# Heads stage of a hybrid attention block: VectorE instead of ScalarE copies the turned probabilities

## Chip, cores and metric

One Trainium2 chip, one of its cores. The metric is the device time of one execution in microseconds (us). The kernel before takes 2724.59 us, the median of 3 runs (2723.51 to 2724.68). The engines are called PE (TensorE), DVE (VectorE), ACT (ScalarE), POOL (GpSimd) and SP (SyncE). PEld is PE's weight load, which overlaps its matmuls.

## The reference, cut to what matters

```python
for start in range(0, S, Q_BLOCK):          # S = 512, Q_BLOCK = 128: four query blocks, b = 0..3
    end = start + Q_BLOCK                   # block b sees 128 * (b + 1) keys
    ...
    # differential heads (8 of them, "kind 0"): two softmaxes and their difference
    p = probs(q1, k1) - lam * probs(q2, k2)
    outs.append(jnp.einsum('bhqk,bhkd->bhqd', p.astype(v.dtype), v[:, :, :end]))
    ...
    # forgetting heads (8 of them, "kind 1"): one softmax
    p = jax.nn.softmax(logits, axis=-1)
    outs.append(jnp.einsum('bhqk,bhkd->bhqd', p.astype(v.dtype), v[:, :, :end]))
```

Around this stand the input projection with RMS norms of queries and keys (`h @ w_in`, then `rms_norm` per head), the gates, the branch projections, the output projection and an MLP. All is float32, 512 tokens by 2048 features.

## The kernel before, in words

The kernel is a chain of stages. In each of them PE multiplies with float32 weights that were split into a rounded high part (by ACT) and a remainder (by DVE), as three products. This case is about the heads stage, from about 490 us to 1010 us of the span.

**Turns and units.** The stage has eight turns (`heads_turn`, a Python call for turn 0 and a hardware loop for turns 1 to 7) and a tail that has the same shape. A turn computes queries and keys of one differential and one forgetting head: 16 units (u = 0 to 15), each of 12 matmuls of 128x512 (L1678, L1680, L1681). The weights of a unit pass through one of four slots: `round_unit` on ACT (L671, once PE has used the slot four units before), `split_unit` on DVE (L1109), then the unit on PE. ACT and DVE prepare unit u+3 in step u.

**Steps of the heads, hung between the units.** `head_hooks` adds to each unit the steps of the heads that are under way. The differential head of turn i has its steps t = 0 to 31 in units 0 to 15 of turn i and 0 to 15 of turn i+1; the forgetting head of turn i has t = 0 to 7 in units 8 to 15 of turn i and t = 8 to 23 in turn i+1. So in unit u of a turn, the head before (differential) is at t = u+16, the head before (forgetting) at t = u+8, and the new differential head at t = u. On every engine the order is the one written out: there is no planner, and each engine takes its instructions strictly in that order.

For query block b of a head the steps are:
- PE `take_scores` (L1723; L1728 and L1730 for the differential head) at SOFTMAX_STEPS[b] = 14, 15, 17, 19, into the PSUM banks `scores`.
- DVE `take_logits` in the same step: adds the bias and takes the row minimum (L1185, after a small memset L1182).
- ACT exponential in the same step (L698).
- DVE `take_probs` one step later (reciprocal L1198; L1201 and L1204 for a differential head, L1207 for a forgetting head).
- PE `turn_probs` at TURN_STEPS (16, 17, 20, 22 for differential and 16, 17, 19, 21 for forgetting heads): b+1 transposes of 128x128 into the one PSUM bank `turned` (L1740). It waits for the probabilities, and for the copy of the block before, since there is one bank.
- `keep_turned` in that same step, on ACT (L717): copies 128 x 128(b+1) float32 from `turned` to SBUF, and raises `p_keys_ready`.
- PE multiplies with the values at PV_STEPS (23 and 22), after the copies of all four blocks (L1778: four matmuls of 512, 384, 256 and 128 columns, each of which the trace records as two).

**Norms.** The new head's queries and keys are normed in the same units: squares on ACT (L678), turned on PE (L1689), reduced on DVE (L1143), a chain of 12 small dependent instructions on DVE (`rsqrt`, L1126 to L1132), widened on PE (L1705), multiplied on DVE (L1167). For the differential head, ACT then rounds (L733) and DVE splits (`split_step`, L1248: two halves for queries, four for keys); PE's first scores of the head (t = 14) wait for that.

**Order within one step on DVE**: products with the widened norm (`scale_step`), then `head_step` of the three heads, then `split_step`, `split_unit`, and at last `norm_step` (reduction and chain). Inside `head_step`, all `take_probs` come first, then for b = 0 to 3 `take_logits(b)`.

**Order within one step on PE**: the heads' hooks come ahead of the unit: for one head, the norm's turns, then scores, then `turn_probs`, then the product with the values.

Of the kernel before, what the change touches and what calls it, by code (L numbers as in the profile page):

```python
# [22 lines left out]
ACT = mybir.ActivationFunctionType  # L23
ALU = mybir.AluOpType

P = 128
# [8 lines left out]
TURN_STEPS = ((16, 17, 20, 22), (16, 17, 19, 21))  # L35
# [14 lines left out]
def at_least(eng, sem, value):  # L50

    if not (isinstance(value, int) and value <= 0):
        eng.wait_ge(sem, value)
# [29 lines left out]
def tile(tensor, m):  # L83

    return tensor[:, m] if isinstance(m, int) else tensor[:, bass.ds(m, 1)].rearrange("p a s -> p (a s)")
# [12 lines left out]
def build(nc, x, w_in, b_forget, w_branch_diff, w_branch_fox, w_gate, w_out, w_mlp_up, w_mlp_down,  # L98
          x_tiles, columns, out):
    _, S, D = x.shape  # L100
    assert x.shape[0] == 1 and w_in.shape[0] == 1 and S == 512
    DT = D // P
    TB = S // P
# [38 lines left out]
    with ExitStack() as ctx:  # L142
# [84 lines left out]
        with ExitStack() as third:  # L227
# [31 lines left out]
        p_blocks = [main_flat[:, p_at + P * b:p_at + P * b + p_stride * (b + 1)].rearrange("p (j c) -> p j c", c=p_stride)  # L259
                    for b in range(TB)]  # L260
# [15 lines left out]
        turned = ctx.enter_context(nc.psum_tensor("turned", [P, S], F32))  # L276
# [384 lines left out]
        def _(act):  # L661
# [22 lines left out]
            def head_step(kind, i, t, work):  # L684

                if t == BIAS_STEP and kind == 1:

                    act.wait_ge(f_wide, i + 1)
                    for b in range(TB):
                        nc.scalar.activation(bias_fox[:, bias_at[b]:bias_at[b + 1]], scores[1][:, 0:P * (b + 1)],  # L690
                                             ACT.Identity, scale=-1.0,
                                             bias=neg_f[:, b, bass.ds(i, 1)]).then_inc(bias_open, 1)
                for b, when in enumerate(SOFTMAX_STEPS):
                    if t == when:
                        block_no = i * (2 * TB) + TB * kind + b
                        act.wait_ge(logits_ready, block_no + 1)
                        for m in range(2 - kind):
                            e = nc.scalar.activation(logits[m][:, 0:P * (b + 1)], logits[m][:, 0:P * (b + 1)],  # L698
                                                     ACT.Exp, scale=-1.0, bias=row_min[:, m:m + 1],
                                                     accum_out=row_sum[:, m:m + 1])  # L700
                        e.then_inc(exp_ready, 1)
                if kind == 1 and t == 22:

                    act.wait_ge(pv_ready, i * 2 + 2)
                    nc.scalar.activation(tile(b_hi, i + H), heads_out[:, :], ACT.Copy).then_inc(o_hi, 1)
                for b in range(TB):
                    if t == TURN_STEPS[kind][b]:
                        keep_turned(kind, i, b)

            def keep_turned(kind, i, b):  # L710


                block_no = i * (2 * TB) + TB * kind + b
                act.wait_ge(probs_turned, block_no + 1)

                at_least(act, pv_ready, i * 2 + kind)
                nc.scalar.activation(p_blocks[b][:, :, 0:P],  # L717
                                     turned[:, 0:P * (b + 1)].rearrange("p (j q) -> p j q", q=P),
                                     ACT.Copy).then_inc(p_keys_ready, 1)

            def norm_step(kind, i, t, work):

# [164 lines left out]
            def heads_turn(i, work):  # L887
                for u in range(HU):
                    round_unit(work, u + LEAD)
                    if isinstance(i, int) and i == 0 and u == 2:  # L890
                        act.wait_ge(lam_sums, 1)
                        nc.scalar.activation(lam[:, 2:4], stats[:, 0:2], ACT.Exp).then_inc(lam_exps, 1)

                        act.wait_ge(f_neg, 1)
                        nc.scalar.activation(lf_t[:, 2], lf_t[:, 1], ACT.Exp).then_inc(f_exp, 1)
                        act.wait_ge(f_one, 1)
                        nc.scalar.activation(lf_t[:, 1], lf_t[:, 2], ACT.Ln).then_inc(f_ln, 1)
                    head_hooks(norm_step, u, i, work)
                    head_hooks(head_step, u, i, work)
# [201 lines left out]
        def _(dve):  # L1101
# [68 lines left out]
            def take_logits(kind, i, b):  # L1170

                block_no = i * (2 * TB) + TB * kind + b
                n = P * (b + 1)
                if kind == 0:
                    dve.wait_ge(dist_ready, i + 5)
                else:
                    dve.wait_ge(bias_ready, i * TB + b + 1)

                at_least(dve, probs_ready, block_no)
                dve.wait_ge(scores_ready, block_no + 1)  # L1180

                nc.vector.memset(pause[:, :], 0.0)  # L1182
                for m in range(2 - kind):
                    bias = spare[:, S - n:S] if kind == 0 else bias_fox[:, bias_at[b]:bias_at[b + 1]]
                    r = nc.vector.tensor_tensor_reduce(out=logits[m][:, 0:n], in0=scores[m][:, 0:n], in1=bias,  # L1185
                                                       scale=1.0, scalar=3e38, op0=ALU.add, op1=ALU.min,
                                                       accum_out=row_min[:, m:m + 1])
                r.then_inc(logits_ready, 1)

            def take_probs(kind, i, b):  # L1190

                block_no = i * (2 * TB) + TB * kind + b
                n = P * (b + 1)
                dve.wait_ge(exp_ready, block_no + 1)

                at_least(dve, probs_turned, block_no - 1)
                count = 2 - kind
                nc.vector.reciprocal(row_inv[:, 0:count], row_sum[:, 0:count]).then_inc(inv_ready, 1)  # L1198
                dve.wait_ge(inv_ready, block_no + 1)
                if kind == 0:  # L1200
                    nc.vector.tensor_scalar(logits[1][:, 0:n], logits[1][:, 0:n], row_inv[:, 1:2], lam_col,  # L1201
                                            ALU.mult, ALU.mult).then_inc(second_scaled, 1)
                    dve.wait_ge(second_scaled, i * TB + b + 1)
                    nc.vector.scalar_tensor_tensor(probs[b % 2][:, 0:n], logits[0][:, 0:n], row_inv[:, 0:1],  # L1204
                                                   logits[1][:, 0:n], ALU.mult, ALU.subtract).then_inc(probs_ready, 1)
                else:
                    nc.vector.tensor_scalar(probs[b % 2][:, 0:n], logits[0][:, 0:n], row_inv[:, 0:1], None,  # L1207
                                            ALU.mult).then_inc(probs_ready, 1)

            def head_step(kind, i, t, work):  # L1210
                if kind == 1 and t == 8:

                    dve.wait_ge(neg_f_ready, 1)
                    nc.vector.tensor_copy(f_repeated.rearrange("p (b c) -> p b c", b=TB),
                                          neg_f[:, :, bass.ds(i, 1)].broadcast_to([P, TB, P])
                                          ).then_inc(f_by_tokens, 1)
                for b, when in enumerate(SOFTMAX_STEPS):
                    if t == when + 1:
                        take_probs(kind, i, b)
                for b, when in enumerate(SOFTMAX_STEPS):  # L1220
                    if t == when:
                        take_logits(kind, i, b)
                if kind == 1 and t == 23:
                    dve.wait_ge(o_hi, i * 2 + 2)
                    nc.vector.tensor_tensor(tile(b_lo, i + H), heads_out[:, :], tile(b_hi, i + H).bitcast(F32),
                                            ALU.subtract).then_inc(o_ready, 1)
                if kind == 0 and t == NORM_STEPS[0][2] + NORM_LENGTHS[0][2] + 1:
                    dve.wait_ge(o_hi, i * 2 + 1)
                    nc.vector.tensor_tensor(tile(b_lo, i), v_feat, tile(b_hi, i).bitcast(F32),
                                            ALU.subtract).then_inc(o_ready, 1)  # L1230
# [850 lines left out]
```

## Time and profile before

| | |
|---|---|
| median of 3 runs | 2724.59 us |
| the profiled execution | 2724.22 us, its span 2722.5 us |
| PE busy | 2694.6 us (99%) |
| DVE busy | 1712.4 us (63%) |
| ACT busy | 1179.3 us (43%) |
| a turn of the heads stage | about 60 us |

How to read it: the span is the stretch between the first and the last instruction in the trace; 1.7 us of the execution lie around it. PE is busy for nearly all of the span, and its granted clock is full. The other engines have idle time everywhere, so a longer or shorter busy time of theirs is not by itself a longer or shorter kernel. In the timeline a start is in us from the span's start; the number after it is the duration in us, except in the groups by line, where a mean or a minimum/median/maximum is in ns. In square brackets stands how long the engine was idle ahead of the instruction and what it inferred to have ended the wait.

### The profile page before, as it was taken

How to read it: one execution, taken by the hardware profiler on the slowest of the kernel's cores; microseconds unless marked ns; L12 is line 12 of the kernel's file. 1: busy time of each engine (PE TensorE's matmuls, PEld its weight loads, DVE VectorE, ACT ScalarE, POOL GpSimd, SP SyncE). 2: the span in 40 equal slices, each digit the busy share in tenths (PEclk: the TensorE clock that was granted, in tenths of full speed). 3: DMA queues.
4: the chain of work that ended last, by engine and by line, in shares of the span. 5: the costliest groups of instructions: out<-in, count | busy, mean ns of one | idle time of the engine just before them, and what ended most of it. 6: DMA issues, size and time to landing. Idle time of an engine off the chain costs nothing.

```text
span 2722.5 us, 44406 instructions
## 1 busy us (share of the span) xinstructions
PE 2694.6 (99%) x15942; PEld 2395.5 (88%) x15942; DVE 1712.4 (63%) x2977; ACT 1179.3 (43%) x1627; POOL 41.3 (2%) x60
## 2 busy tenths in 40 slices
PE   8999999999999999999999999999999999999999
PEld 6999999788888888888899999999998888888887
DVE  4538887577777754434488878788864444444444
ACT  5534443455555552223444444444444333433342
POOL 0000000010000000000000000000000000000000
PEclk9999999999999999999999999999999999999999
DMA  6343443423223235444434343433356565565653
GB/s 241 111 130 125 130 129 115 111 78 85 76 74 85 81 100 148 139 131 149 130 117 131 123 139 123 134 128 131 131 180 229 193 217 195 198 224 186 228 196 116
DMA packets 359556, 386.96 MB, mean 142 GB/s; under 512 B 16448, under 2 KB 273984, under 8 KB 358976
## 3 DMA queue, kind: packets, MB, share of 16 engines
q1 hardware_dynamic: 331920, 347.24, 40.4%
q10 hardware_dynamic: 27568, 38.81, 4.0%
q8 instruction: 43, 0.70, 0.1%
q14 instruction: 25, 0.20, 0.0%
HBM read 348.23 MB, written 37.75 MB: 142 GB/s over the span
## 4 chain that ended last, share of the span: by engine, by line
PE 96%; DVE 1%; DMA 1%; ACT 1%; issue 0%; SPq 0%; ACTq 0%; DVEq 0%
PE job L1678 7%; PE job L1681 7%; PE job L1680 7%; PE scores L1987 2%; PE job L1987 2%; PE job L1991 2%; PE job L1989 2%; PE scores L1989 2%; PE scores L1991 2%; PE job L2014 2%; PE job L2016 2%; PE job L2015 2%; PE scores L2014 2%; PE scores L2015 2%; PE scores L2016 2%; PE heads_out L1778 1%
## 5 line engine op out<-in xcount | busy, mean ns | idle before, releaser
L1615 DVE TENSOR_TENSOR w_lo_d<-raw_d,w_hi_d 128x512 fp32r<-128x512 f32 x256 | 176.3, 690 | 368.9 <-ACT w_hi_d L1054 368.9
L1354 DVE TENSOR_TENSOR lo<-pair,hi 128x1792 fp32r<-128x1792 f32 x142 | 287.3, 2023 | 125.0 <-ACT hi L832 125.0
L832 ACT ACTIVATE hi<-pair 128x1792 fp32r<-128x1792 f32 x142 | 241.5, 1701 | 271.9 <-PE heads_out L1991 118.5
L1054 ACT ACTIVATE w_hi_d<-raw_d 128x512 fp32r<-128x512 f32 x256 | 161.4, 632 | 405.0 <-PE heads_out L2016 202.8
L671 ACT ACTIVATE w_hi<-raw 128x512 fp32r<-128x512 f32 x272 | 171.0, 631 | 365.2 <-PE job L1681 247.3
L1109 DVE TENSOR_TENSOR w_lo<-raw,w_hi 128x512 fp32r<-128x512 f32 x272 | 190.0, 700 | 171.7 <-ACT w_hi L671 166.0
L1678 PE MATMUL job<-a_hi,w_hi 128*128 128x512 f32 x576 | 236.2, 410 | 3.0 <-DVE w_lo L1109 3.0
L1681 PE MATMUL job<-a_hi,w_lo 128*128 128x512 f32 x576 | 225.9, 392 | 0.0
L1680 PE MATMUL job<-a_lo,w_hi 128*128 128x512 f32 x576 | 224.8, 390 | 0.0
L1987 PE MATMUL scores<-h,hi 128*128 128x256 f32 x512 | 145.5, 284 | 4.7 <-DVE h L1547 2.6
L1621 DVE TENSOR_TENSOR u_lo<-u_raw,u_hi 128x2048 fp32r<-128x2048 f32 x64 | 146.2, 2285 | 4.0 <-ACT u_hi L1060 4.0
L1991 PE MATMUL scores<-h,lo 128*128 128x256 f32 x512 | 145.3, 284 | 0.0
L1989 PE MATMUL scores<-h,hi 128*128 128x256 f32 x512 | 145.3, 284 | 0.0
L1987 PE MATMUL job<-h,hi 128*128 128x256 f32 x512 | 144.9, 283 | 0.0
L1991 PE MATMUL job<-h,lo 128*128 128x256 f32 x512 | 144.9, 283 | 0.0
L1989 PE MATMUL job<-h,hi 128*128 128x256 f32 x512 | 144.9, 283 | 0.0
L1681 PEld LDWEIGHTS job<-a_hi,w_lo 128*128 128x128 f32 x576 | 108.0, 188 | 24.3
L1678 PEld LDWEIGHTS job<-a_hi,w_hi 128*128 128x128 f32 x576 | 108.4, 188 | 23.5 <-issue 1.9
L1680 PEld LDWEIGHTS job<-a_lo,w_hi 128*128 128x128 f32 x576 | 108.6, 189 | 19.5
L1060 ACT ACTIVATE u_hi<-u_raw 128x2048 fp32r<-128x2048 f32 x64 | 121.7, 1902 | 7.7 <-DMA u_raw<-u_rows 7.7
L1344 DVE TENSOR_TENSOR pair<-pair 128x512 f32<-128x512 f32 x170 | 116.4, 685 | 0.0
L1268 DVE TENSOR_TENSOR w_lo<-raw,w_hi 128x344 fp32r<-128x344 f32 (+1 forms) x80 | 46.8, 589 | 92.9 <-ACT w_hi L779 92.9
(449 smaller groups left out, 7734.6 us busy)
## 6 DMA issues: line engine op xcount, KB each, us to landing
pair<-in_w_mlp_up SPq DMA_DIRECT2D x256, 256.0 KB, 2.8
u_raw<-u_rows SPq DMA_DIRECT2D x64, 1024.0 KB, 5.6
raw_d<-in_w_mlp_down SPq DMA_DIRECT2D x128, 512.0 KB, 6.1
raw<-in_w_in SPq DMA_DIRECT2D x80, 512.0 KB, 4.1
pair<-in_w_gate SPq DMA_DIRECT2D x84, 256.0 KB, 2.9
raw<-in_w_out SPq DMA_DIRECT2D x64, 256.0 KB, 3.3
u_rows<-u_out ACTq DMA_DIRECT2D x32, 512.0 KB, 4.3
raw<-in_w_in SPq DMA_DIRECT2D x24, 344.0 KB, 3.2
```

Of the source, the lines that this page charges most:

```text
L671: nc.scalar.activation(w_hi[:, u % SPLITS], raw[:, slot, part:part + KU], ACT.Copy).then_inc(hi_ready, 1)
L832: nc.scalar.activation(pair_hi[j % 2], pairs[j][:, :, 1:8], ACT.Copy).then_inc(pair_hi_ready, 1)
L1054: nc.scalar.activation(w_hi_d[:, j % SPLITS], raw_d[:, j // 2, j % 2], ACT.Copy).then_inc(down_hi, 1)
L1109: nc.vector.tensor_tensor(w_lo[:, u % SPLITS], raw[:, slot, part:part + KU], w_hi[:, u % SPLITS].bitcast(F32), ALU.subtract).then_inc(spli ...
L1354: nc.vector.tensor_tensor(pair_lo[j % 2], pairs[j][:, :, 1:8], pair_hi[j % 2].bitcast(F32), ALU.subtract).then_inc(pair_lo_ready, 1)
L1615: nc.vector.tensor_tensor(w_lo_d[:, j % SPLITS], raw_d[:, j // 2, j % 2], w_hi_d[:, j % SPLITS].bitcast(F32), ALU.subtract).then_inc(down_ ...
L1678: nc.tensor.matmul(result[:, :], w_hi[:, slot, k], act_hi[:, f], start=(n == 0 and k == 0), stop=False)
L1680: nc.tensor.matmul(result[:, :], w_hi[:, slot, k], act_lo[:, f], start=False, stop=False)
L1681: done = nc.tensor.matmul(result[:, :], w_lo[:, slot, k], act_hi[:, f], start=False, stop=(n == units - 1 and k == KU - 1))
L1987: nc.tensor.matmul(into, high, h_slices[s][:, a, 0], start=first, stop=False, skip_group_check=True)
L1989: nc.tensor.matmul(into, high, h_slices[s][:, a, 1], start=False, stop=False, skip_group_check=True)
L1991: done = nc.tensor.matmul(into, low, h_slices[s][:, a, 0], start=False, stop=(j == 3 and k == 1), skip_group_check=True)
```

## The change

`keep_turned` moves from ACT to DVE. It becomes `nc.vector.tensor_copy` with the same source, target and semaphores, and DVE does the waits. Its place in DVE's order is inside `head_step`, in the same steps as before (TURN_STEPS), in the loop over b and behind `take_logits` of the same b: so in a step where block b is turned and block b+1 has its logits taken (differential t = 17; forgetting t = 17 and t = 19), the copy of block b stands ahead of the logits of block b+1. Nothing else is changed, on PE neither.

```diff
@@ ACT head_step @@
-                for b in range(TB):
-                    if t == TURN_STEPS[kind][b]:
-                        keep_turned(kind, i, b)
-
-            def keep_turned(kind, i, b):
-                block_no = i * (2 * TB) + TB * kind + b
-                act.wait_ge(probs_turned, block_no + 1)
-                at_least(act, pv_ready, i * 2 + kind)
-                nc.scalar.activation(p_blocks[b][:, :, 0:P],
-                                     turned[:, 0:P * (b + 1)].rearrange("p (j q) -> p j q", q=P),
-                                     ACT.Copy).then_inc(p_keys_ready, 1)
@@ DVE @@
+            def keep_turned(kind, i, b):
+                block_no = i * (2 * TB) + TB * kind + b
+                dve.wait_ge(probs_turned, block_no + 1)
+                at_least(dve, pv_ready, i * 2 + kind)
+                nc.vector.tensor_copy(p_blocks[b][:, :, 0:P],
+                                      turned[:, 0:P * (b + 1)].rearrange("p (j q) -> p j q", q=P)
+                                      ).then_inc(p_keys_ready, 1)
+
             def head_step(kind, i, t, work):
...
                 for b, when in enumerate(SOFTMAX_STEPS):
                     if t == when:
                         take_logits(kind, i, b)
+                    if t == TURN_STEPS[kind][b]:
+                        keep_turned(kind, i, b)
```

## Rows read from the trace of the kernel before

**Rows 1.** The page: busy time per engine, and the chain that ended last, by engine.
```profile
PE 2694.6 (99%) x15942; PEld 2395.5 (88%) x15942; DVE 1712.4 (63%) x2977; ACT 1179.3 (43%) x1627; POOL 41.3 (2%) x60
PE 96%; DVE 1%; DMA 1%; ACT 1%; issue 0%; SPq 0%; ACTq 0%; DVEq 0%
```
**Rows 2.** PE's waits from 480 to 1080 us: total, times, longest.
```profile
PE job L1678 <- DVE w_lo L1109: 3.0, 2, 1.5
PE heads_out L1860 <- DVE lf L1432: 0.8, 1, 0.8
PE scores L1728 <- DVE k_lo L1248: 0.7, 1, 0.7
```
**Rows 3.** One turn by windows: busy us per engine, PE's clock, DMA.
```profile
740.00:800.00 60.00, 60.00 (x297) 48.88 (x296) 45.59 (x155) 31.51 (x70) 4.17 (x5) 1.00 0.29 79
```
**Rows 4.** The copies by line: ns min/median/max, first and last start.
```profile
L717 ACT ACTIVATE main<-turned x64: 257/414/582, 534.5 to 1001.3; 128x128 f32<-128x128 f32 x16, 128x256 f32<-128x256 f32 x16, 128x384 f32<-128x384 f32 x16, 128x512 f32<-128x512 f32 x16
```
**Rows 5.** DVE groups by line and shape: busy us, mean ns, idle before.
```profile
L1185 DVE CUSTOM_DVE_ANT_0 side<-scores,spare 128x512 f32<-128x512 f32 x16 | 10.4, 687 | 7.5 <-issue 7.5
L1185 DVE CUSTOM_DVE_ANT_0 side<-scores,spare 128x384 f32<-128x384 f32 x16 | 8.3, 556 | 0.0
L1185 DVE CUSTOM_DVE_ANT_0 side<-scores,spare 128x256 f32<-128x256 f32 x16 | 6.2, 422 | 0.0
L1185 DVE CUSTOM_DVE_ANT_0 side<-scores,spare 128x128 f32<-128x128 f32 x16 | 4.0, 287 | 0.0
L1450 DVE COPY main<-heads_out 8x512 f32<-8x512 f32 x1 | 0.7, 679 | 0.8 <-PE heads_out L1860 0.8
L1214 DVE COPY main<-neg_f 128x512 f32 x7 | 2.9, 421 | 0.0
```
**Rows 6.** Timeline: unit 9 to unit 11 of a steady turn.
```profile
747.77 0.38 PE L1740 MATMUL turned<-ident,side 128*128 128x128 f32 x2
747.98 0.55 DVE L1185 CUSTOM_DVE_ANT_0 side<-scores,main 128x384 f32<-128x384 f32 x1 [1.66 <-issue]
...
754.41 0.42 DVE L1207 TENSOR_SCALAR side<-side,row_inv 128x384 f32<-128x384 f32 x1
754.88 0.14 PEld L1740 LDWEIGHTS turned<-ident,side 128*128 128x128 f32 x1 [0.35 <-DVE side L1207]
755.20 0.49 PE L1740 MATMUL turned<-ident,side 128*128 128x128 f32 x3
```
**Rows 7.** Timeline of DVE: 128x512 logits, the second right behind the first.
```profile
785.44 0.69 DVE L1185 CUSTOM_DVE_ANT_0 side<-scores,spare 128x512 f32<-128x512 f32 x1 [0.99 <-issue]
...
786.05 0.69 DVE L1185 CUSTOM_DVE_ANT_0 side<-scores,spare 128x512 f32<-128x512 f32 x1
```
**Rows 8.** Timeline: unit 12 to unit 14 of the same turn.
```profile
758.93 0.69 DVE L1167 TENSOR_TENSOR main<-main,wide 128x512 f32<-128x512 f32 x1 [2.22 <-PE wide L1705]
...
761.49 0.60 PE L1740 MATMUL turned<-ident,side 128*128 128x128 f32 x4
...
763.75 0.17 DVE L1132 SCALAR_TENSOR_TENSOR stat<-stat 128x8 f32<-128x8 f32 x1
764.03 2.79 DVE L1248 TENSOR_TENSOR k_lo<-main,b_lo 64x512 fp32r<-64x512 f32 x4
...
765.03 0.30 PEld L1778 LDWEIGHTS heads_out<-main 128*128 128x128 f32 x2
...
767.18 0.19 PEld L1728 LDWEIGHTS scores<-b_lo,b_hi 128*128 128x128 f32 x1
```
**Rows 9.** The same place in turn 0: DVE's last piece (chain of work), and PE.
```profile
526.02 0.70 DVE k_lo L1248
...
526.77 0.39 PE L1728 MATMUL scores<-b_lo,b_hi 128*128 128x256 f32 x1 [0.72 <-DVE k_lo L1248]
```
**Rows 10.** Timeline: units 1 and 2 of the next turn.
```profile
779.48 0.17 DVE L1132 SCALAR_TENSOR_TENSOR stat<-stat 128x8 f32<-128x8 f32 x1
779.97 0.06 DVE L1182 MEMSET pause<- 128x1 f32 x1 [0.32 <-DVE stat L1132]
...
780.48 0.58 PEld L1705 LDWEIGHTS wide<-ident,stat 128*128 128x128 f32 x4
```
**Rows 11.** Timeline of DVE: where it waits in units 7 and 8.
```profile
741.26 0.42 DVE L1185 CUSTOM_DVE_ANT_0 side<-scores,main 128x256 f32<-128x256 f32 x1 [0.90 <-DVE side L1207]
...
744.57 0.69 DVE L1167 TENSOR_TENSOR main<-main,wide 128x512 f32<-128x512 f32 x1 [2.28 <-PE wide L1705]
```

## The prediction, made before the changed kernel was timed

> **What bounds the kernel now.** I read the page first: PE is busy for 2694.6 of 2722.5 us, and the chain that ended last is 96% PE [rows 1]. DVE at 63% and ACT at 43% have room on average, but an average says nothing about a single wait, so the waits of PE came next. In the whole heads stage and a little beyond, PE waited 4.5 us, all of it in the first turn and its surroundings (4 waits) [rows 2]; in a steady turn PE is busy for the full 60.00 us, DVE for 45.6, ACT for 31.5 [rows 3]. Two things follow. The change can win nothing in the turns where the copies are, because nothing there waits for ACT: taking load from ACT only makes its idle time longer. And whatever the added DVE work delays in PE's stream is added to the end in full, since every stage behind is PE's too and has no wait that could shrink. So the question is where DVE is nearly late for PE, and for that I walked through the timeline of one turn, 740 to 800 us, DVE beside PE.
>
> **What goes, what comes.** Off ACT: 64 copies of 257 to 582 ns [rows 4], about 26.5 us (64 x the median of 414 ns), hidden before. Worth 0. On to DVE: 64 copies, 16 of each length. The trace has hardly a plain DVE copy from PSUM. The nearest rows are the logits, DVE from PSUM with full width: 287, 422, 556 and 687 ns for 128 to 512 columns [rows 5]. The one copy from PSUM, 512 columns on 8 partitions, took 679 ns; a copy of 512 columns inside SBUF took 421 [rows 5]. I take the logits' figures, because source memory and width agree and the PSUM copy confirms the longest; the SBUF copy (0.61 of it) is the lower end. That is 16 x (0.287+0.422+0.556+0.687) = 31.2 us of DVE, 3.9 per turn: 45.6 becomes 49.5 of 60. In an unbroken stream a DVE instruction costs less than its duration: the second logits started 0.61 us after the first, which lasts 0.69 [rows 7]. So I charge 0.21, 0.35, 0.48 and 0.61.
>
> Trainium skill, "VectorE: DVE Perf Modes", section "Why PSUM operands drop a tier": a float32 source in PSUM runs at one element per cycle, while copies within SBUF may run at two. The trace's pair of 679 and 421 ns agrees [rows 5]; without it the sum would be the low end given below. The same page, "The DRAIN you can't avoid", says that the next DVE instruction does not start until the pipe is empty. That would charge the whole 0.69 for a copy of 512 columns, 0.08 more in each of the two places below, or about 1.1 us more over the stage. The 0.61 between starts speaks against it [rows 7].
>
> **Weights.** DVE splits unit u+3 in step u, so a delay of some tenths never reaches a unit. A copy's wait for PE's transposes does not cost either in most steps, since DVE must wait for PE in the neighbouring steps anyway. DVE idles 0.9 and 2.3 us in units 7 and 8 [rows 11], 1.66 in unit 9 [rows 6], 2.2 at unit 12 [rows 8] and 1.0 in unit 3 [rows 7]. These waits cut the turn into segments; a delay made in one is gone at the next. Only PE's own deadlines inside a segment count. I find two that are tight.
>
> **Place A, unit 9 to the turn of block 2 of the forgetting head (unit 11).** Before, DVE starts the logits of block 2 at 747.98, when PE's scores are there. Now the copy of block 1 stands ahead of them, in the loop over b, and it waits for transposes that end at 747.77+0.38 = 748.15 [rows 6]. Copy from 748.2, logits 0.35 later, at 748.55: 0.55 late. From there DVE has no pause through the query split, the weight split and the chain of the norm to the probabilities of block 2, which end at 754.41+0.42 = 754.83; PE's weight load for the turn follows at 754.88, and its matmul at 755.20, when the array is free [rows 6]. With 0.55 more the load starts at 755.43 and takes 0.14 [rows 6], so the transposes come between 755.43 and 755.57: PE loses 0.23 to 0.37. I take 0.30.
>
> **Place B, unit 12 to the first scores of the next differential head (unit 14).** DVE starts again with PE at 758.93 after an idle of 2.2 us [rows 8], so what A delayed has moved with PE. The chain of the norm ends at 763.92; the key split of four pieces follows at 764.03 and ends at 766.82; PE loads for the scores at 767.18 [rows 8]. The copy of block 3, 512 columns, now comes between chain and key split. Its transposes were done at 762.1, so there is no wait for PE. But behind a chain, waits cost: 0.11 us ahead of the key split with one wait [rows 8], 0.32 ahead of the memset with three [rows 10]; for the copy's two I take 0.21, so 0.10 more than now. Key split later by 0.10+0.61 = 0.71, end at 767.53. In turn 0, where PE did wait here, it began 0.05 after the key split's end (526.72 to 526.77) [rows 9]; so 767.58 against 767.18, a loss of 0.40. The product with the values, which needs this copy, loads at 765.03 [rows 8]; the copy ends at 764.82, just in time, and a slip there would be taken off the later wait.
>
> **Next in line, place C.** Behind B, DVE is 0.71 late and the copy of block 0 in unit 0 adds 0.21, while PE is 0.40 late. The chain of unit 1's norm ends at 779.65+0.92 = 780.57; PE's load for widening it comes at 780.48+0.40 = 780.88 [rows 10]. Spare 0.3. The copy of block 1 behind it ends in DVE's idle 1.0 at unit 3 [rows 7].
>
> **Sum.** Both places exist where a forgetting head meets the next differential head: turns 1 to 7, seven times (the tail has no new head, and turn 0 has no copies). 7 x (0.30+0.40) = 4.9 us. Against the profiled execution's 2724.22 (span 2722.5 plus 1.7 around it) that is 2729.1; the median of the runs is 0.4 above the profiled one, so 2729.5.
>
> **Bounds.** Low: copies at the SBUF rate and no extra wait. A is 0.40 late and costs about 0.15, B 0.34 late and costs about 0.03: 1.3 us, so 2725.9. High: each wait of DVE costs 0.3 more than counted in; A 0.5, B 0.6, C 0.3, or 1.4 per turn: 9.8 us, so 2734.4. Below nothing is excluded but for tenths, since PE has no wait in these turns [rows 3].
>
> **Rivals.**
> 1. Hidden. DVE's slack is larger than it looks, for instance because PE's starts at 755.20 and 767.18 are modelled and the array was in truth free later. For it: DVE has 14 us of idle per turn. Against: PE's load at 754.88 already waits for DVE (0.35) [rows 6]. Time 2724.6, chance 0.12.
> 2. Only one of A and B costs (the copy is nearer its low end, or PE's array hides the load). 2726.7 to 2727.4, chance 0.13.
> 3. The other side, slower beyond doubt: place C decides too. If copies and their waits put DVE 0.3 us per turn later than reckoned between the key split and unit 1's norm, PE's widening waits as well, and the same excess enters A and B. From that point each tenth counts up to three times: 0.50+0.55+0.15 = 1.2 per turn, 8.4 us, so 2733.0. For it: the price of waits behind a chain rests on two gaps. Against: most of the copies run in a stream where waits are covered. Chance 0.17.
> 4. Faster. ACT's freed time brings rounded weights earlier, and PE's 3.0 us of waits for weights vanish [rows 2]. They lie in turn 0, where there are no copies, so this gives nothing even then; 2724 or a little below, chance 0.03.
>
> The change does what it says: engine and place are plain in the code, so I give no chance to the contrary.
>
> **How the numbers follow.** The two places together, as summed, have 0.55, spread from 2727.5 to 2732. No change means within 0.2%, which is 5.4 us: up to 2730.0, about what a measurement of this kernel can tell apart. The forecast is just inside; of its 0.55 some 0.28 lie below that bound and 0.27 above. Same: 0.28 + 0.12 + 0.13 = 0.53, rounded to 0.52; slower: 0.27 + 0.17 = 0.44, rounded to 0.45; faster 0.03. The range from 2725.6 to 2734.0 leaves out most of rival 1 and 4 and the far end of rival 3.
>
> **What the profile after would show.** DVE copies from `turned` of about 0.29, 0.42, 0.55 and 0.68 us; DVE at about 49.5 of 60 us per turn; each of turns 1 to 7 about 0.7 us longer. In PE's waits two rows that are new, seven times each: L1740 for DVE's probabilities of 384 columns (about 0.3 each) and L1728 for the key split (about 0.4 each). No new wait of a unit (L1678) for `w_lo`. A wait of L1705 for the chain means place C. I am wrong if the waits are absent (rival 1), if L1678 waits for weights in every turn, or if the difference lies outside 560 to 1000 us.

## The result: 2738.6 us, slower by 14.6 us, and the profile after

| | before | after |
|---|---|---|
| median of 6 runs | 2723.97 us | 2738.58 us |
| profiled execution's span | 2722.5 us | 2736.4 us |
| ratio, 95% interval | | 1.0054 [1.0041, 1.0067] |
| PE / DVE / ACT busy | 2694.6 / 1712.4 / 1179.3 us | 2699.3 / 1739.1 / 1157.8 us |

The forecast was 2729.5 us with a range to 2734.0. The change costs three times what was forecast, and lies outside the range.

In the kernel after, `keep_turned` is at L1202 on DVE, and lines behind it are shifted (`turn_probs` L1738, `widen` L1703, the reciprocal L1184, the chain L1112 to L1118, first scores L1726, key split L1246, `split_unit` L1095). The page of the kernel after, with the two queues that load instructions:

```profile
PE 2699.3 (99%) x15942; PEld 2394.1 (87%) x15942; DVE 1739.1 (64%) x3041; ACT 1157.8 (42%) x1563; POOL 37.0 (1%) x60
...
q8 instruction: 43, 0.70, 0.1%
q14 instruction: 55, 0.45, 0.1%
...
PE 89%; DVE 6%; issue 2%; DMA 1%; ACT 1%; DVEq 0%; ACTq 0%; SPq 0%
```

The chain of work has 2% of "issue", where it had none [rows 1]: time in which an engine waits for nothing that the profile shows. And queue q14 has 55 packets; the page of before has this line:

```profile
q14 instruction: 25, 0.20, 0.0%
```

So 30 more packets of code, 0.25 MB, though DVE's compiled program has only 31 instructions more. Below, edits to DVE's program alone take this count to 55 (f2) and back to 25 (f1), so q14 is DVE's queue. PE's waits from 480 to 1100 us, against [rows 2]:

```profile
PE wide L1703 <- DVE stat L1118: 5.7, 6, 1.0
PE turned L1738 <- DVE main L1202: 3.4, 6, 0.8
PE job L1676 <- DVE w_lo L1095: 1.4, 1, 1.4
PE heads_out L1858 <- DVE lf L1430: 0.8, 1, 0.8
PE scores L1726 <- DVE k_lo L1246: 0.7, 1, 0.7
```

Two new rows, six times each. Neither is the row that I named for A or B: PE waits for the norm's chain (my place C), and for a copy that has to free `turned`. One step upstream, DVE's own waits from 480 to 1030 us name the source:

```profile
DVE main L1202 <- PE turned L1738: 18.5, 17, 2.9
DVE row_inv L1184 <- issue: 16.1, 6, 2.9
```

The second is new: before, the same reciprocal waited 3.3 us six times in all, put down to PE. The timeline of DVE and ACT around it, at the end of unit 15 and the start of unit 0 of the next turn, kernel after:

```profile
778.81 0.69 DVE L1095 TENSOR_TENSOR w_lo<-raw,w_hi 128x512 fp32r<-128x512 f32 x1
...
779.84 0.19 ACT L698 ACTIVATION_READ_ACCUMULATOR side<-side,row_min 128x1 f32 x1
...
782.13 0.17 DVE L1184 RECIPROCAL row_inv<-row_sum 128x2 f32<-128x2 f32 x1 [2.64 <-issue]
...
783.61 0.41 PE L1738 MATMUL turned<-ident,side 128*128 128x128 f32 x2 [0.51 <-DVE main L1202]
```

and before, the same reciprocal, whose input ACT finished as far behind the start of the weight split as after, 1.22 us:

```profile
773.22 0.69 DVE L1109 TENSOR_TENSOR w_lo<-raw,w_hi 128x512 fp32r<-128x512 f32 x1
774.47 0.17 DVE L1198 RECIPROCAL row_inv<-row_sum 128x2 f32<-128x2 f32 x1 [0.56 <-PE turned L1740]
```

All that the reciprocal needs is there at 779.84+0.19 = 780.03, but it starts at 782.13: 2.1 us for which no semaphore accounts. Between the weight split and the reciprocal stands one thing only, the jump back to the start of the hardware loop. The rows of DVE's sequencer (DVEq in the profile, where jumps, waits and register instructions are listed) show it: the jump, then the first instruction behind it. After, then before:

```profile
L1457 DVEq COMPARE_BRANCH  x1: 68/68/68, 778.7 to 778.7; - x1
L1457 DVEq FUSED_REGOPS  x1: 78/78/78, 781.9 to 781.9; - x1
```
```profile
L1459 DVEq COMPARE_BRANCH  x1: 56/56/56, 772.9 to 772.9; - x1
L1459 DVEq FUSED_REGOPS  x1: 74/74/74, 773.2 to 773.2; - x1
```

After, 3.2 us lie between them; before, 0.3. Part of the 3.2 is hidden, because DVE still has its weight split to do and then waits for ACT in any case; 2.1 us are left. The DMA view of the kernel after from 775 to 785 us shows three packets of code in that stretch (40 slices of 0.25 us; the isolated 33s from the 17th slice on are they):

```profile
GB/s 0 0 0 61 115 113 158 303 336 348 332 264 64 4 0 0 33 0 33 0 0 0 0 0 0 0 0 0 0 0 33 0 0 0 0 0 0 0 0 0
...
q14 instruction: 3, 0.02, 0.8%
```

In the trace each packet has 8192 bytes, and the three start at 779.09, 779.73 and 782.72. The first two are right behind the jump at 778.7. In a steady turn of the kernel before, 700 to 760 us, this view has none.

The length of a turn comes from the queue row of one ACT line that runs once per turn (first and last of seven, so six turns lie between). Before, then after:

```profile
L705 ACTq FUSED_REGOPS  x7: 46/46/46, 588.2 to 948.8; - x7
```
```profile
L705 ACTq FUSED_REGOPS  x7: 51/51/51, 586.2 to 961.5; - x7
```

360.6/6 = 60.10 us before, 375.3/6 = 62.55 after: 2.45 us more per turn, where the prediction had 0.70. The starts of PE's instructions in the two traces (mean of three steady turns) say where: 1.11 us more ahead of the widening (place C), 0.88 between scores and transposes (place A has 0.22 of it, the turn of block 1 behind the jump 0.66), 0.25 at place B, and 0.13 among the widenings and transposes.

### The profile page after: what moved, and what is told of

Read it like the earlier page. It is cut to its first block, busy times and chain, and to the rows that moved or that the text cites. A ratio compares the mean times of both kernels' runs of the same rounds, so it can differ in the third digit from the quotient of the medians.

```text
span 2736.4 us, 44398 instructions
## 1 busy us (share of the span) xinstructions
PE 2699.3 (99%) x15942; PEld 2394.1 (87%) x15942; DVE 1739.1 (64%) x3041; ACT 1157.8 (42%) x1563; POOL 37.0 (1%) x60
## 4 chain that ended last, share of the span: by engine, by line
PE 89%; DVE 6%; issue 2%; DMA 1%; ACT 1%; DVEq 0%; ACTq 0%; SPq 0%
PE job L1676 5%; PE job L1679 5%; PE job L1678 5%; PE scores L1985 2%; PE job L1985 2%; PE job L1989 2%; PE job L1987 2%; PE scores L1989 2%; PE scores L1987 2%; PE job L2012 2%; PE job L2014 2%; PE job L2013 2%; PE scores L2012 2%; PE scores L2013 2%; PE scores L2014 2%
## 5 line engine op out<-in xcount | busy, mean ns | idle before, releaser
L1095 DVE TENSOR_TENSOR w_lo<-raw,w_hi 128x512 fp32r<-128x512 f32 x272 | 188.7, 696 | 169.3 <-ACT w_hi L671 163.7
```

The lines of the kernel that those rows point to most:

```text
L1095: nc.vector.tensor_tensor(w_lo[:, u % SPLITS], raw[:, slot, part:part + KU], w_hi[:, u % SPLITS].bitcast(F32), ALU.subtract).then_inc(spli ...
```

## The experiments

Theory now: the pause is the loading of code. With the copies, DVE's loop reaches into a further block of the instruction stream, and after each jump back its start has to be loaded again. Its rivals: the loop is too long wherever it lies; or DVE is late from the copies and their waits, and "issue" is only how that shows. I counted instructions in DVE's compiled program, from its first one: start and end of the heads loop, start counted at the branch ahead of it. In time order of the runs ("moved by n" is n memsets on DVE ahead of the loop, each of one column of a tile added for it, in a wait for a DMA):

| kernel | loop from, to (length) | packets on q14 | DVE pause at the jump | us per turn | against before |
|---|---|---|---|---|---|
| before | 451, 735 (284) | 25 | none | 60.10 | |
| after | 451, 751 (300) | 55 | 16.1 us in 6 | 62.55 | +14.6 |
| e1: after, moved by 16 | 467, 767 (300) | 55 | 12.3 in 6 | 61.73 | +9.8 |
| e2: before, 9 memsets in the loop | 451, 744 (293) | 25 | none | 60.12 | +0.2 |
| e3: after, DVE's turns written out | no loop | 33 | none | 60.70 | +4.6 |
| e4: as e1, A and B undone | 467, 765 (298) | 55 | 12.1 in 6 | 60.97 | +5.5 |
| f1: after, moved by 48 | 499, 799 (300) | 25 | none | 60.78 | +5.3 |
| f2: before, moved by 16 | 467, 751 (284) | 55 | 16.2 in 6 | 61.75 | +10.1 |
| f3: as f1, A and B undone | 499, 797 (298) | 25 | none | 60.23 | +1.4 |
| f4: as f1, A undone | 499, 799 (300) | 26 | none | 60.55 | +3.5 |
| g1: before, moved by 48 | 499, 783 (284) | 25 | none | 60.25 | +1.0 |
| g2: before, moved by 12 | 463, 747 (284) | 55 | 18.7 in 6 | 62.05 | +12.2 |
| g3: as f1, B undone | 499, 797 (298) | 25 | none | 60.45 | +3.3 |

"Against before" is the difference of the medians, with the kernel before measured beside each. The pause column is the total and count of waits put down to "issue" ahead of the reciprocal behind the jump; each contains 0.56 us of real waiting for ACT. In every kernel with "none" and a loop, DVE's sequencer needs 0.28 to 0.35 us from the jump to the next instruction; in every other one 2.8 to 3.7. The turns are good to about 0.02 us.

**e1, the changed kernel moved by 16.**

```diff
+            for z in range(16):
+                nc.vector.memset(filler[:, z:z + 1], 0.0)
             dve.wait_ge(g_stored, 32 * GATE_PAIRS)
```

> The changed kernel with 16 one-column memsets on DVE ahead of the heads loop, in a stretch where DVE waits for a DMA anyway; the loop's code is the same, only its place in DVE's instruction stream moves by 16. Theory 'code position': the 2.1 us pause of DVE at each of six jumps back to the loop's start is code that has to be loaded again because the loop, nine instructions longer, reaches into one more block of code; moved by 16 it fits again, the six pauses vanish, and only places A and B are left (measured 0.22 + 0.26 us per turn, seven times, 3.4 us): about 2727.5. Theory 'code length' (the loop is too long wherever it lies): about 2738.5, pauses stay. Theory 'DVE is late from the copies themselves': about 2738.5 too, and the pause stays.

2732.72 against 2722.94 us (1.0037 [1.0023, 1.0051]). The pauses stay, but are shorter: each 2.0 us instead of 2.6.

```profile
780.07 0.17 DVE L1185 RECIPROCAL row_inv<-row_sum 128x2 f32<-128x2 f32 x1 [2.02 <-issue]
```

A move of code alone, with the same loop, gave back a third of the loss. That speaks for position, but the pauses were to vanish and did not: a miss, since I had not placed the edge rightly.

**e2, nine more instructions in the loop of before.**

```diff
                 for u in range(HU):
+                    if u == 8 and not first:
+                        for z in range(9):
+                            nc.vector.memset(filler[:, z:z + 1], 0.0)
                     head_hooks(scale_step, u, i, work)
```

> The kernel before (ACT copies) with nine one-column memsets on DVE inside the heads loop, in unit 8, where DVE idles 2.3 us: the loop is as long, and lies where, it does in the changed kernel. Code position and code length both: a pause of about 2 us at six jumps; DVE's norm chain of unit 1 then ends 2.1 us later against a spare of 0.8 us, PE loses about 1.3 us per turn, 8 us in all: about 2732. DVE late from the copies: no pause, 2724.

2723.11 (1.0001 [0.9992, 1.001]), no pause. A miss for both code theories as written; only the third, that DVE is late from the copies, had foretold it. The reason was my count: a copy with two waits that must both be waited for brings instructions of its own for them. The compiled loop of after has 300 instructions and not the 293 of this kernel. So 293 instructions, ending at 744, do no harm.

**e3, DVE's seven turns written out.**

```diff
-            with dve.Fori(1, H) as i:
+            for i in range(1, H):
                 heads_turn(i, Work(HEADS.unit, HEADS.job, i, HU, HJ))
```

> The changed kernel with DVE's turns 1 to 7 written out one after the other instead of a hardware loop; the other engines keep their loops. Code position and code length: no jump, so no pause of about 2 us, places A and B remain: about 2727.5 (if loading code in a straight line costs something too, more). DVE late from the copies: 2738.5, since the work is the same.

2727.57 (1.0017 [1.0008, 1.0026]): +4.6 us, with the same 64 copies on DVE. So the copies with their waits cost about 4.6 and the jump the other 10. Straight-line code needs 8 packets more than before, and they cost nothing that is seen. The theory that DVE is late from the copies alone falls here: the work is the same, and 10 us are gone.

**e4, moved by 16, A and B undone.** `take_logits` comes first, and ACT keeps block 3 of the forgetting heads (DVE's part of the edit):

```diff
-                    if t == TURN_STEPS[kind][b]:
-                        keep_turned(kind, i, b)
+                for b in range(TB):
+                    if t == TURN_STEPS[kind][b] and (kind, b) != (1, TB - 1):
+                        keep_turned(kind, i, b)
```

> As the first of these four (moved by 16), and besides the copy stands behind the logits of the next block (place A undone) and ACT keeps the copy of block 3 of the forgetting heads (place B undone); DVE still does 56 of 64 copies. Code position, with A and B as the only other costs: as the kernel before, 2724 to 2724.5. If the moved copies cost PE elsewhere too (place C): 2726 or more. Code length: about 2735.

2728.44 (1.002 [1.001, 1.003]). The 2724 to 2724.5 expected of position was a miss, as in e1: the move by 16 does not end the pause (12.1 us), which costs 5.5 here. A and B undone took 4.3 off e1.

**f1, moved by 48** (as e1, with 48 memsets).

> The changed kernel, the heads loop's code moved by 48 instead of 16 instructions (one-column memsets on DVE ahead of it). In DVE's compiled program, counted from its first instruction, the loop ran from 452 to 751 in the changed kernel and from 468 to 767 in the one moved by 16 (both pause at the jump); it ran from 452 to 735 before and to 744 with the nine memsets inside (no pause). Now 500 to 799. Theory 'code position': a loop pauses if it reaches into three blocks of code, and one edge lies shortly behind 744 and at or before 751, the edge below it 256 lower; moved by 48 the loop starts behind the lower edge and lies in two blocks: no pause, places A and B remain, about 2726.5 to 2727.5. Theory 'code length' (300 instructions are too many, 293 are not): the pauses stay, 2732 or more.

2728.37 (1.0021 [1.0012, 1.003]). No pause, the packets back at 25, 9.3 us of the 14.6 gone, with 48 useless instructions more; that is 0.9 to 1.9 above what was expected for A and B alone (g1 below has 1.0 of it). Length 300 is harmless there; the length theory falls.

**f2, the kernel before moved by 16.** No copy is moved; this is the cleanest of the tests.

> The kernel before (ACT copies, loop of 284 instructions) moved by 16: the loop runs from 468 to 751. Code position: it now reaches over the edge between 744 and 751, so DVE pauses about 2 us at each of six jumps although nothing else is changed, and PE loses about 0.9 to 1.3 us of each at the widening of unit 2: about 2729 to 2731. Code length: 284 is below every loop that paused, so no pause, 2723.

2733.18 (1.0035 [1.0022, 1.0049]): +10.1 us for 16 memsets outside the loop that lie in a wait. Its waits of DVE (480 to 1030 us) and its queue row have what the changed kernel has:

```profile
DVE row_inv L1199 <- issue: 16.2, 6, 3.0
...
q14 instruction: 55, 0.45, 0.1%
```

PE waits for the norm's chain, as in the kernel after, now without any copy on DVE:

```profile
PE wide L1708 <- DVE stat L1133: 6.6, 6, 1.1
```

I had expected 2729 to 2731, because I charged PE only with the wait at `widen` (1.1 per turn); the turn grew by 61.75-60.10 = 1.65. By the starts of PE's instructions 1.26 us more lie ahead of the widening, 0.11 among widenings and transposes and 0.08 between scores and transposes. The last 0.15 lie between the matmuls of the units, and g1 below, which has no pause, has them too; why is open.

**f3 and f4, moved by 48 with A and B undone, and with A undone.**

> Moved by 48, the copy behind the logits of the next block (A undone), block 3 of the forgetting heads copied by ACT (B undone); DVE does 56 of 64 copies. Code position with A and B as the only other costs: 2723 to 2723.5, as the kernel before. Code length: about 2728.

2724.42 (1.0004 [0.9995, 1.0013]).

> Moved by 48 with only place A undone, all 64 copies on DVE. If A and B are as the changed kernel's timeline has them (0.22 and 0.26 us per turn, seven turns): 1.5 us less than the first of these four and 1.8 us more than the third, about 2725. If the two are not independent (a stall at A gives DVE time that it lacks at B), this one is no faster than the first.

2726.55 (1.0013 [1.0004, 1.0022]): 1.8 us less than f1, and 2.1 more than f3, where 1.5 and 1.8 were expected. So the two places do not depend on each other.

**g1, control: before moved by 48.**

> Control for the moved kernels: the kernel before (ACT copies) moved by 48, its loop from 499 to 783. Code position: the loop starts behind the lower edge and lies in two blocks again, no pause, 2723 like the kernel before; the 48 memsets fall into a wait for a DMA. If memsets or the moved later stages cost something, it shows here and must be taken off the figures of the other kernels moved by 48.

2724.02 (1.0003 [0.9994, 1.0013]): no pause, and a time that can't be told from the kernel before. Against this control f3 has nothing left (+0.4, and 60.23 against 60.25 us per turn): with A and B undone, 56 copies on DVE cost nothing that these runs resolve.

**g2, the edge: before moved by 12.**

> The kernel before moved by 12: the loop ends at 747, between the last end without a pause (744) and the first with one (751). Code position with an edge at one place: either like the kernel before (2723, 25 packets of code on DVE's queue) or like the one moved by 16 (about 2733, 55 packets), nothing between. A cost that grows with the size of what crosses would give about 2725.

2735.2 (1.0047 [1.0032, 1.0063]). An end at 747 gives the full effect, one at 744 none: an edge, no slope. The pause is even longer, 3.0 us.

**g3, B undone.**

> Moved by 48 with only place B undone (ACT copies block 3 of the forgetting heads, DVE the other 56, ahead of the next block's logits). Both undone gave +1.4 us, only A undone +3.5, none undone +5.3. If A and B add up, this one is at about 1.4 + 1.8 = +3.2 us, near 2726.3; per turn 60.1 + 0.13 + 0.23 = 60.45 us.

2726.29 (1.0012 [1.0003, 1.0021]). As expected. Per turn A is 60.78-60.55 = 0.23 us and B is 60.78-60.45 = 0.33, together 0.56 against the 0.55 between f1 and f3: they add up. Measured from the other end, A is 60.45-60.23 = 0.22 and B 60.55-60.23 = 0.32.

## Why the prediction was wrong, point by point

**The step that failed.** It is a term that the sum does not have, put at nothing without a reason: what the copies do to DVE's own loop of code. The prediction says of DVE's delays that "a delay made in one is gone at the next" and that "Only PE's own deadlines inside a segment count", and works these out as if an instruction cost only what its row in the trace says. Eight copies in the loop also are 16 instructions more in DVE's compiled loop (284 to 300). That pushed its end from 735 over an edge between 744 and 747, and each of the six jumps back then costs DVE a pause of 2.1 us (timeline above) and PE about 1.8, in all 9 to 10 of the 14.6 us. Shown by f2 and g2 (the pause with no copy moved), f1 (the copies with no pause) and e3 (the copies with no jump). The queue row for loaded code, 25 packets to 55, is five more per jump.

The Trainium skill has this, in "Runtime: NRT & Kernel Launch", section "Instruction fetch mechanics": code comes in blocks of 16 KiB, 256 instructions, two of them held at a time, fetched in sequence; a taken branch to a block no longer held waits for a DMA. The runs agree: the loop of 284 instructions pauses or not by position alone. They put the upper edge between 744 and 747, if one edge serves for e2 and g2, and the lower one between 467 and 499: a loop that passes the upper edge pauses if it starts at 451, 463 or 467, and doesn't if it starts at 499. With the page's block of 256 the lower edge would be between 488 and 491, inside that stretch, and the loops that pause would be those that touch three blocks; no run narrows it further. The page calls straight-line code preferable; e3 bears it out here (+4.6 instead of +14.6). The pause is measured: 2.0 to 3.3 us as the profile's idle time gives it.

**A wait of 2.1 us became about 1.8 us per turn.** 62.55-60.78 = 1.77 between after and f1, 62.55-60.70 = 1.85 between after and e3. DVE leaves the jump 2.1 us late, and the prediction had worked out "Spare 0.3" for place C, which fits. So nearly all of it reaches PE, at the turn of block 1 (wait 0.51 in the timeline) and at the widening (0.95). Place C, which decides in rival 3, was the right place; rival 3 had the copies and their waits as its cause, and 2733.0 as its time, and both were wrong.

**The price of a copy: right.** Groups by line and shape of the kernel after, against the 287, 422, 556 and 687 ns taken from [rows 5]:

```profile
L1202 DVE COPY main<-turned 128x512 f32<-128x512 f32 x16 | 11.0, 690 | 2.6 <-PE turned L1738 2.3
L1202 DVE COPY main<-turned 128x384 f32<-128x384 f32 x16 | 8.8, 551 | 3.2 <-PE turned L1738 2.9
L1202 DVE COPY main<-turned 128x256 f32<-128x256 f32 x16 | 6.8, 424 | 12.7 <-PE turned L1738 12.4
L1202 DVE COPY main<-turned 128x128 f32<-128x128 f32 x16 | 4.6, 287 | 1.5 <-PE turned L1738 0.8
```

31.2 us together, as summed: a copy of 512 columns from PSUM takes 690 ns, against 421 inside SBUF [rows 5]. DVE's busy time grew by 26.7 us only, because rows that overlap are counted once (the copy of 512 columns below and the split behind it start 0.61 apart, as charged), and ACT's fell by 21.5, not 26.5.

**Place A: right place and mechanism, 0.22 to 0.23 instead of 0.30 us per turn.** Kernel after, unit 9 to 11:

```profile
752.84 0.42 DVE L1202 COPY main<-turned 128x256 f32<-128x256 f32 x1 [1.49 <-PE turned L1738]
753.19 0.55 DVE L1171 CUSTOM_DVE_ANT_0 side<-scores,main 128x384 f32<-128x384 f32 x1
...
759.00 1.02 PE L1721 MATMUL scores<-main 128*128 128x512 f32 x2
...
760.08 0.31 PEld L1738 LDWEIGHTS turned<-ident,side 128*128 128x128 f32 x3 [0.89 <-DVE side L1193]
```

The logits start 0.35 behind the copy, as charged. From PE's scores to its transposes it is 1.08 us: the matmuls of the turn start at 760.08 as well. Before it was 0.86: the turn at 755.20 [rows 6], and the scores in this row of before:

```profile
754.34 1.02 PE L1723 MATMUL scores<-main 128*128 128x512 f32 x2
```

**Place B: right place and mechanism, about 0.3 instead of 0.40.** Kernel after, unit 13 and 14, against [rows 8]:

```profile
768.69 0.17 DVE L1118 SCALAR_TENSOR_TENSOR stat<-stat 128x8 f32<-128x8 f32 x1
768.89 0.69 DVE L1202 COPY main<-turned 128x512 f32<-128x512 f32 x1
769.50 2.78 DVE L1246 TENSOR_TENSOR k_lo<-main,b_lo 64x512 fp32r<-64x512 f32 x4
...
769.96 0.30 PEld L1776 LDWEIGHTS heads_out<-main 128*128 128x128 f32 x2
...
772.40 0.19 PEld L1726 LDWEIGHTS scores<-b_lo,b_hi 128*128 128x128 f32 x1 [0.21 <-issue]
```

The copy began 0.03 us after the chain, not 0.21: the extra price for waits behind a chain was wrong. The key split began 0.64 behind the chain's end at 768.86, where it had begun 0.11 behind: 0.53 late instead of 0.71. PE's load for the scores comes 2.44 us behind its load for the product with the values, before 2.15 [rows 8], so 0.29 are lost; by the turns of f1 and g3 it is 0.33.

**The two places together** made 0.55 us per turn, 3.9 in seven turns, and 2728.37-2724.42 = 4.0 between the medians of f1 and f3; forecast 4.9. (f1 as a whole is 5.3 above before, and 0.68 per turn; but g1, moved by 48 and with no copy on DVE, has 1.0 and 0.15 of that.) So the two terms of the sum came out a fifth smaller than forecast, and the whole excess over the forecast is the jump.

**What I said would show it wrong** did not fully catch it: the difference lies between 560 and 1000 us and no unit waits for weights in every turn. The two rows foretold for PE's waits, seven times each, are missing, and yet A and B cost: even in f1, without the pause, PE waits by the profile for the key split only twice (1.0 us), and for the probabilities not at all. Their cost shows in the distances between PE's starts. The row foretold for place C is there. The sign of the jump was the "issue" row of DVE.

**The rivals.** "Hidden" and "only one of A and B" fall by f4 and g3, since each place alone costs. "Faster" falls. "Nothing waits for ACT" held: the ACT time taken off brought nothing.

**When the code is loaded.** In each of the five kernels that pause, five packets of 8192 bytes start in a turn. In the kernel after they start about 27 us ahead of the jump, and 0.4, 1.0, 4.0 and 9.4 us behind it, so more is loaded again than the loop's start. The first of those four moves with the loop's end: it starts 0.6 us behind the jump in g2 (end at 747), 0.4 behind in the kernel after and in f2 (751), about 2.8 ahead of it in e4 (765) and 3.9 ahead in e1 (767). The next one starts 1.0 to 1.3 behind in all. The time from the jump to the next instruction is 3.5 us in g2, 3.2 in the kernel after and f2, 2.8 in e1 and e4. That fits a load which begins when the end of the loop crosses the edge, so that a longer way from edge to jump hides more of it. It was not tested by itself, and why a turn brings just five packets stays open.

## What to carry to other kernels

An instruction added to a hardware loop has a price beyond its duration: the loop can cross an edge of loaded code and then pay at every jump. Count instructions in the compiled program, waits included, and look at the packets of the instruction queue, at "issue" waits behind the jump and at the sequencer's rows around it. Fillers ahead of the loop tell this cause from others, if they are enough to carry it past an edge: 48 ended the pause here, 16 did not, and 12 brought it about in the kernel before. And a timing in a kernel with long hardware loops that moves by some us is to be doubted until the loops' positions are controlled: f2 lost 10.1 us by sixteen no-work memsets, more than the 4.6 that the copies cost in e3.

## What the runs showed of the hardware that I had not expected

- The pause: DVE's sequencer needs 3.2 us for a jump instead of 0.3 in the kernel after, of which 2.1 reach DVE, with 2 packets of code of 8192 bytes right behind the jump.
- The edge is sharp: an end at 744 costs 0.2 us, one at 747 12.2 us over six jumps.
- A DVE copy behind a chain of dependent small instructions, with two waits of its own, started 0.03 us after it. The 0.11 and 0.32 us seen before [rows 8, 10] are no price of waits that can be carried over.
